# A hybrid attention and expert backbone on one core: the softmax's normalisation moves from the probabilities into the matrix of their transposes

## What is computed

```python
def mla_attend(q_nope, q_rope, k_nope, k_rope, v):
    s = (jnp.einsum('bqhd,bkhd->bhqk', q_nope, k_nope)
         + jnp.einsum('bqhr,bkr->bhqk', q_rope, k_rope))
    p = jax.nn.softmax(s.astype(jnp.float32) * ATTN_SCALE, axis=-1).astype(v.dtype)
    return jnp.einsum('bhqk,bkhd->bqhd', p, v)
```

## Time and profile before

| | |
|---|---|
| median of three executions | 1306.02 us (1305.56 to 1306.17) |
| the profiled execution | 1304.85 us |
| its span | 1302.1 us |
| mean granted TensorE clock | 0.998 |
| busy TensorE / VectorE / ScalarE / GpSimd | 98% / 33% / 17% / 1% |
| DMA | 459.68 MB, mean 353 GB/s |

### The profile page before, as it was taken

The page is one execution under the profiler, slowest core; times in us unless marked ns, Lnnn a source line. Parts: engine busy times, 40 slices in busy tenths (PEclk is TensorE's granted clock), DMA queues, the critical chain, the costliest instruction groups (busy, mean ns, idle before and its releaser), DMA issues.

```text
span 1302.1 us, 28096 instructions
## 1 busy us (share of the span) xinstructions
PE 1282.2 (98%) x12471; PEld 660.4 (51%) x12471; DVE 433.9 (33%) x867; ACT 225.4 (17%) x386; POOL 17.3 (1%) x34
## 2 busy tenths in 40 slices
PE   8999999999999999999999999999999999999997
PEld 7757999999994333333333333433333333333333
DVE  4588699999753010300111020111102002011203
ACT  4374534343441000000000000000000000000002
POOL 0400000000000000000000000000000000000000
PEclk9999999999999999999999999999999999999999
DMA  9953799897575879999999999999899999999980
GB/s 390 380 197 138 288 383 353 333 356 305 197 286 240 363 311 412 420 376 402 422 420 371 410 421 374 403 409 378 343 412 421 376 400 421 411 385 410 420 349 34
DMA packets 60835, 459.68 MB, mean 353 GB/s; under 512 B 6960, under 2 KB 7344, under 8 KB 9392
## 3 DMA queue, kind: packets, MB, share of 16 engines
q1 hardware_dynamic: 60720, 457.92, 86.8%
HBM read 456.78 MB, written 1.11 MB: 352 GB/s over the span
## 4 chain that ended last, share of the span: by engine, by line
PE 80%; DVE 13%; issue 2%; DMA 2%; ACT 2%; SPq 0%; DVEq 0%; ACTq 0%
PE bank L2208 44%; PE bank L2221 22%; DVE work L1075 6%; DVE split L1059 4%; PE bank L1760 4%; DMA ring<-in_mixa 1%; PE bank L1832 1%; PE bank L2188 1%; PE bank L2178 1%; PE bank L1652 1%; DMA ring<-in_mixout 1%; PE bank L1968 1%; DVE ring L1348 1%; DVE split L1359 1%; DVE work L1073 0%
## 5 line engine op out<-in xcount | busy, mean ns | idle before, releaser
L2208 PE MATMUL bank<-ring,work 128*32 128x512 f32 (+1 forms) x6144 | 584.9, 539 | 1.1 <-DVE moe L1584 1.1
L2208 PEld LDWEIGHTS bank<-ring,work 128*32 128x32 f32 x6144 | 199.2, 110 | 377.3 <-issue 344.2
L2221 PE MATMUL bank<-ring,moe 128*32 128x512 f32 x2688 | 294.1, 592 | 0.0
L1584 DVE TENSOR_TENSOR moe<-moe,bank 128x256 f32<-128x256 f32 (+1 forms) x96 | 31.5, 383 | 658.4 <-ACT moe L970 658.4
L2221 PEld LDWEIGHTS bank<-ring,moe 128*32 128x32 f32 x2688 | 87.4, 110 | 197.6 <-issue 196.3
L970 ACT ACTIVATE moe<-bank 128x256 f32<-128x256 f32 (+1 forms) x96 | 27.4, 357 | 792.3 <-PE bank L2208 792.3
L2053 PE MATMUL bank<-split 128*128 128x256 f32 x1024 | 125.4, 283 | 0.8 <-DVE split L1059 0.7
L2053 PEld LDWEIGHTS bank<-split 128*128 128x128 f32 x1024 | 123.7, 192 | 1.6 <-DVE split L1059 1.2
L1059 DVE TENSOR_TENSOR split<-ring,split 128x2048 fp32r<-128x2048 f32 x33 | 75.5, 2289 | 6.3 <-ACT split L875 3.0
L1075 DVE SCALAR_TENSOR_TENSOR work<-ring,condp,work 128x512 f32<-128x512 f32 x98 | 73.7, 752 | 4.1
L875 ACT ACTIVATE split<-ring 128x2048 fp32r<-128x2048 f32 x31 | 59.4, 1915 | 73.0 <-PE bank L2053 70.7
(11 more groups left out here) (259 smaller groups left out, 613.2 us busy)
## 6 DMA issues: line engine op xcount, KB each, us to landing
ring<-in_moe SPq DMA_DIRECT2D x336, 1024.0 KB, 13.5
ring<-in_ffn SPq DMA_DIRECT2D x16, 2048.0 KB, 8.3
ring<-in_ada SPq DMA_DIRECT2D x28, 1024.0 KB, 7.1
ring<-in_ada SPq DMA_DIRECT2D x10, 2048.0 KB, 9.8
ring<-in_mixout SPq DMA_DIRECT2D x2, 2048.0 KB, 8.4
ring<-in_fnet SPq DMA_DIRECT2D x2, 2048.0 KB, 8.6
ring<-in_mixa SPq DMA_DIRECT2D x2, 1024.0 KB, 15.2
tail<-tables SPq DMA_DIRECT2D x8, 256.0 KB, 17.7
```

The lines of the kernel that those rows point to most:

```text
L1584: nc.vector.tensor_tensor(gate_e[:, g, 0:n], gate_e[:, g, 0:n], bank[g][:, n:2 * n], ALU.mult).then_inc(e_hidden, 1)
L2208: last = mm(bank[g][c * QUAD:(c + 1) * QUAD, 0:count * P], x_group[:, 4 * half + k, j * CAP + g * QUAD:j * CAP + (g + 1) * QUAD], source[: ...
L2221: last = mm(bank[3 + n][c * QUAD:(c + 1) * QUAD, :], hiddenT[phase % 2][:, g, blk * QUAD:(blk + 1) * QUAD], source[:, j, n * 512:(n + 1) * ...
```

## The change

The exponentials in `probs` stay unscaled. `normalised` now multiplies the 128x128 identity by the reciprocals, one for each partition, which gives a diagonal matrix in a new buffer `shares` (four of them; the view lies on columns of `work` that held the rotation tables, whose last reader is earlier). `turn` no longer transposes: it multiplies each tile of exponentials with that diagonal in an ordinary matmul, so the scaling happens while the tile is turned. The semaphore `probs_ready` becomes `shares_ready`. The turn of the ada rows on TensorE moves from item 11 to 12 and its taking on VectorE from 12 to 13; the row copy stays at item 10.

```diff
         rope = view(work, 2560, 2, T)
+        shares = view(work, 2560, 4, P)
...
-        scores_ready, max_ready, exp_ready, probs_ready = (
-            sem("scores_ready"), sem("max_ready"), sem("exp_ready"), sem("probs_ready"))
+        scores_ready, max_ready, exp_ready, shares_ready = (
+            sem("scores_ready"), sem("max_ready"), sem("exp_ready"), sem("shares_ready"))
...
-        ROWS_ITEM, TURN_ITEM, TAKE_ITEM = 10, 11, 12
+        ROWS_ITEM, TURN_ITEM, TAKE_ITEM = 10, 12, 13
...
                 link(nc.vector.reciprocal(small[:, 48 + n:49 + n], small[:, 48 + n:49 + n]))
-                nc.vector.tensor_scalar(probs[:, n % 4, :], probs[:, n % 4, :], small[:, 48 + n:49 + n], None,
-                                        ALU.mult).then_inc(probs_ready, 1)
+                nc.vector.tensor_scalar(shares[:, n % 4, :], C("ident"), small[:, 48 + n:49 + n], None,
+                                        ALU.mult).then_inc(shares_ready, 1)
...
             def turn(n):
-                pe.wait_ge(probs_ready, n + 1)
+                pe.wait_ge(shares_ready, n + 1)
                 if n >= 2:
                     pe.wait_ge(probsT_taken, n - 1)
                 for kt in range(4):
-                    last = nc.tensor.transpose(bank[3 + n % 2][:, kt * P:(kt + 1) * P],
-                                               probs[:, n % 4, kt * P:(kt + 1) * P], C("ident"))
+                    last = mm(bank[3 + n % 2][:, kt * P:(kt + 1) * P], probs[:, n % 4, kt * P:(kt + 1) * P], shares[:, n % 4, :],
+                              start=True, stop=True)
                 last.then_inc(probsT_ready, 1)
```

## The result

The changed kernel took 1308.48 us (median of nine executions, 1307.89 to 1310.26), the kernel before 1305.45 us (median of its now nine, 1303.33 to 1306.17). The ratio is 1.003, with a 95% interval of 1.0021 to 1.0038: slower by 2.7 to 5.0 us. By the means of the same executions (1308.76 and 1305.04) it is 3.7. The forecast was slower, +4.3 us, 1310.3 within 1307.4 to 1312.2.

The account below looks back on a forecast made before the run. TensorE's own length was taken to bound the attention stretch (first score product to output projection, 36.26 us), VectorE second. Turns +7.3 and gaps -3.0 gave +4.3 us, on the median 1306.02 us 1310.3, range 1307.4 to 1312.2.

Parts of the forecast that it names:

- The turn: TensorE's turn of four tiles in each of 16 attention items: 0.44 to 0.90 us, +7.3 us in all.
- The gaps: TensorE's four idle places ahead of turns in the attention stretch, together 3.03 us: all close, -3.0 us.
- The ada turn: TensorE's turn of the ada rows, one item later, starting at 103.5 us: its 1.32 us gap goes.
- VectorE: Its scaling step, 128 columns for 512: 0.24 us, saving 4.0 us over 16, costed at nothing for the time.
- Behind the stretch: From the output projection to the kernel's end: nothing absorbs the shift, so the whole +4.3 us arrives.
- The instructions to fetch: 128 more instructions beside 12471 pairs in the whole kernel, called one in a hundred more, put at zero.
- Fewer slots: Rival: a turn by the diagonal costs no more than transposes, only gaps go: -3.0, 1303.0 us; 5%.
- The gaps stay: Rival: the turn waits for the diagonal or copies move back, all 3.0 us remain: +7.3, 1313.3 us; 7%.
- absorbed: Rival: cheap turns (+2.6) or a late load hiding part of the rest, within 0.2%, 1306.0 to 1308.6 us; 13%.
- Four times the slots: Rival: each plain product as long as four transposes, a turn 1.76 us, sum +18, 1324 us; 2%.

Follow-up runs that it names:

- tensor_only: Changed kernel with the identity in place of the diagonal and VectorE's 128x512 scaling put back; 1308.17 us, 1.0030 of the kernel before.
- move_back: Changed kernel with the ada turn back at item 11 and its taking at 12; 1309.29 us, 1.0038 of the kernel before.
- turn_twice: Changed kernel with each product of a turn made twice into the same columns; 1322.91 us, 1.0136 of the kernel before.
- vector_only: Changed kernel with turns as transposes again and VectorE's diagonal built but unused, normalisation left out; 1303.94 us, 0.9995 of the kernel before.
- move_only: Kernel before with only the ada turn and its taking one item later; 1304.67 us, 0.9998 of the kernel before.
- spread_sums: Against the changed kernel: unscaled exponentials transposed, no diagonal, attend's result scaled for each pair of heads in float32; 1305.26 us, 0.9999 of the kernel before.
- one_pass: Changed kernel with exponentials and diagonals kept in fp32r, one instruction a product; 1303.24 us, 0.9989 of the kernel before.

## Why the prediction was right

- **The turn.** Eight instructions of 0.112 us, 0.90 us a turn, taken from line 1722: measured 0.89. The step is 0.45 for 0.46; 16 x 0.45 = +7.2 us.
- **The gaps.** 3.03 us in four places, all closed: 7.2 - 3.03 = +4.2, measured +4.10. The gaps of items 2, 3, 14 and 15 went as argued; item 3 had the little room that it was given, as tensor_only shows with 0.02 us.
- **The ada turn.** The prediction let the move close that gap. The sum was right, the cause was wrong: move_back has no gap either, since TensorE comes to item 11 late enough by itself. The move could have been costed at zero; here it was luck that the wrong cause gave the right sum.
- **VectorE.** 0.24 us for the new step: measured 0.287. The straight line between one column and 512 was the wrong line. From 128 to 512 columns it is (487 - 287) / 384 = 0.52 ns a column. The Trainium skill (VectorE: DVE Perf Modes, "Mode 2×_2P — use both read ports for one tensor") has operations with one tensor source, source and destination in SBUF, run at two elements a cycle, in float32 too, which at its 0.96 GHz is 0.52 ns an element (an estimate from its figures); the two rows agree. VectorE's work in the stretch fell to 28.20 us and not to about 27. As said, the term is worth nothing to the time: tensor_only has VectorE's old step and the same length.
- **Behind the stretch.** Passed on one to one, by turn_twice and by the fixed distances behind the projection's first product. The one thing that the prediction didn't see, the load of the Fourier mixer's weights, added 0.9 us in the trace of the changed kernel, just under the 1 us at which it called itself wrong there.
- **The instructions to fetch.** 128 more beside 12471 pairs is one in two hundred, not one in a hundred; the term was put at zero either way.
- **The size.** +4.3 was forecast and the interval is 2.7 to 5.0. The 1.8 us between 1310.3 and 1308.48 are not in the turn or the gaps. 0.6 of them is that nine executions gave the kernel before a median of 1305.45 instead of 1306.02, and 0.2 is the stretch, 4.10 us for 4.3. For the rest the records have this: the span from the first to the last instruction has a mean of 1306.9 us over the nine executions of the changed kernel and 1302.8 over the 69 of the kernel before that ran beside the experiments, +4.1 as in the stretch; what lies outside the span is 1.8 us in each of the nine, but 1.7 to 3.1, mean 2.2, in the 69. That takes 0.4 us off the difference in time; why it does isn't shown. That the median came out where it did is in part luck: the time alone would also fit a step of 2.7 us.
- **What moves single executions.** The first score started between 74.7 and 78.1 us in the twelve traces, though nothing ahead of it was changed. TensorE's granted clock early on sets most of that. It was 1.00 from 10 to 20 us in seven of them, six of which have the first score at 74.7 to 75.2; the seventh is vector_only, 77.3, where ScalarE waited 9.2 us instead of 6.5 for the projection's first weights. It was 0.83 in move_only, move_back, turn_twice and spread_sums, 76.3 to 76.6, and 0.59 in one_pass, 78.1. One ada unit in that stretch (line 1652) took 1.96 us in the kernel before and 3.51 in move_only. The same ten microseconds in the kernel before, in move_only and in one_pass:

```profile
10.00:20.00 10.00, 8.25 (x107) 7.15 (x107) 7.44 (x19) 3.83 (x7) 0.00 (x0) 1.00 1.01 427
10.00:20.00 10.00, 8.19 (x95) 6.93 (x94) 6.04 (x18) 3.98 (x7) 0.00 (x0) 0.83 0.99 421
10.00:20.00 10.00, 8.65 (x81) 6.81 (x82) 4.29 (x15) 2.75 (x6) 0.00 (x0) 0.59 1.00 424
```

  The changed kernel's two longest executions, 1309.81 and 1310.26 us, are the two with a mean granted clock of 0.996 where the other seven have 0.999. Why the clock is at its lower level in some executions isn't shown.
- **The rivals.** "Fewer slots" is what one_pass does: it has the change's form and one instruction a product, and is faster, as that rival had it; in plain float32 it doesn't occur. "The gaps stay" and "absorbed" didn't come. "Four times the slots" is out: the plain product is 0.89 / 0.44 = 2.0 transposes long. The Trainium skill (TensorE: Matmul & The Clock Gate, "Terms") has the transpose mode 4x faster for float32; on this row it is twice, and the measurement decides. A transpose's 0.11 us is close to the 0.099 us that line 1857 takes with only 2 moving columns, so a floor of the weight load may hide a larger factor; no run has tiles with which to tell.

## What to carry to other kernels

Before work is folded into a transpose, count instructions: in float32 a transpose of 128x128 is one and a product of the same shape two, and on the engine that sets the pace the second one outweighs anything that it saves on another. Idle time between the groups of the bound engine can't be added up as a gain: take away one wait, and the next link of the chain (here maximum, exponent, copy) holds most of it (0.98 of 1.32 us in move_only); but it can be set against a cost on that engine, where it closes by itself. Small free gains, about 1 us here, lay in where side work stands in VectorE's queue: put it where the bound engine is on something that needs no one, and spread it. Two rows of side work in one place opened new gaps of 0.45 and 0.69 us.

## What the runs showed that was not expected

- The chain of maximum, exponent and copy takes back what a shorter scaling or a removed wait frees: 0.59 us in vector_only and 0.79 in move_only, ahead of the same turn, that of item 9.
- One late load costs more than its wait: in vector_only, 3.16 us of idle TensorE were followed by 6.9 us at a granted clock of 0.52, in which four score instructions took 3.39 us instead of 1.88. The stretch got 3.25 us longer by it (38.19 - 34.94), and that execution took 1308.31 us, where the median of its kernel is 1303.94. The other traces, with idle times of 0.6 to 1.0 us at that point, keep the clock.
